# Entry of a two-block transformer kernel: two narrow weight slots first, and the second token tile normed by VectorE

## The reference, cut to what matters

```python
hn = rms_norm(h, norm_g[0])           # h = x, 512 tokens x 1024
...                                   # hn @ ev_w_in[0], cut in columns: q, k, v, gate, u, gate
u = hn @ ev_w_in[0][:, 1280:1792]     # 512 columns, the input of the state-space part
```

## Time and profile before

| | us |
|---|---|
| median of 3 runs | 1859.51 |
| lowest and highest run | 1858.56, 1860.19 |
| the profiled execution | 1856.27 |
| its span, first to last instruction | 1854.5 |

### The profile page before, as it was taken

The page is one execution under the profiler, slowest core; times in us unless marked ns, Lnnn a source line. Parts: engine busy times, 40 slices in busy tenths (PEclk is TensorE's granted clock), DMA queues, the critical chain, the costliest instruction groups (busy, mean ns, idle before and its releaser), DMA issues.

```text
span 1854.5 us, 24422 instructions
## 1 busy us (share of the span) xinstructions
PE 1780.5 (96%) x9572; PEld 1409.0 (76%) x9572; DVE 960.3 (52%) x1928; ACT 513.7 (28%) x1144; POOL 1015.7 (55%) x1051
## 2 busy tenths in 40 slices
PE   7778899999899999999999999999999999999998
PEld 6565668767668877778888888887667798888886
DVE  5849575488453345443564156434566356514642
ACT  3430453321442344442111021122434321101111
POOL 7406145656316574335776677655343377667762
PEclk9889899999999999999999999999999999999999
DMA  6121311322123321112332333222112133233321
GB/s 183 35 69 46 114 46 55 117 69 80 40 69 115 102 92 51 64 47 67 112 108 86 100 105 91 80 91 91 46 46 69 46 105 112 85 95 105 91 94 54
DMA packets 173058, 151.68 MB, mean 82 GB/s; under 512 B 9304, under 2 KB 148056, under 8 KB 172944
## 3 DMA queue, kind: packets, MB, share of 16 engines
q1 hardware_dynamic: 172400, 149.69, 26.5%
q10 hardware_dynamic: 544, 0.44, 0.1%
HBM read 147.97 MB, written 2.14 MB: 81 GB/s over the span
## 4 chain that ended last, share of the span: by engine, by line
PE 86%; DVE 5%; ACT 1%; issue 1%; DVEq 0%; ACTq 0%
PE ps L279 72%; PE ps L1932 2%; PE ps L1965 2%; PE ps L1950 2%; PE ps L1431 1%; PE ps L350 1%; PE ps L1409 1%; DVE s_tmp L1110 1%; PE ps L1908 1%; PE ps L1938 1%; PE ps L1352 1%; PE ps L1360 1%; PE ps L1368 0%; PE ps L1421 0%; PE ps L741 0%
## 5 line engine op out<-in xcount | busy, mean ns | idle before, releaser
L127 POOL TENSOR_SCALAR w_hi<-w_raw 128x512 fp32r<-128x512 f32 x522 | 314.7, 629 | 795.7 <-PE ps L279 732.8
L131 POOL TENSOR_TENSOR w_lo<-w_raw,w_hi 128x512 fp32r<-128x512 f32 x522 | 695.6, 1364 | 11.2
L279 PE MATMUL ps<-x_hi,w_hi 128*128 128x512 f32 (+1 forms) x1448 | 539.1, 372 | 0.7 <-DVE x_lo L432 0.7
L279 PE MATMUL ps<-x_hi,w_lo 128*128 128x512 f32 (+1 forms) x1448 | 528.9, 365 | 0.0
L279 PE MATMUL ps<-x_lo,w_hi 128*128 128x512 f32 (+1 forms) x1448 | 528.7, 365 | 0.0
L279 PEld LDWEIGHTS ps<-x_hi,w_hi 128*128 128x128 f32 x1448 | 275.3, 190 | 71.3 <-issue 21.7
L279 PEld LDWEIGHTS ps<-x_hi,w_lo 128*128 128x128 f32 x1448 | 275.1, 190 | 44.1
L279 PEld LDWEIGHTS ps<-x_lo,w_hi 128*128 128x128 f32 x1448 | 275.5, 190 | 40.5 <-issue 0.5
L2226 DVE SCALAR_TENSOR_TENSOR ffn_cv<-ps,col,ffn_cv 128x510 f32<-128x510 f32 (+1 forms) x176 | 131.8, 749 | 192.8 <-ACT ffn_cv L2204 188.1
L2204 ACT ACTIVATE ffn_cv<-ps,col 128x512 f32<-128x512 f32 x88 | 63.7, 775 | 500.2 <-PE ps L279 500.2
L307 DVE TENSOR_TENSOR h<-h,ps 128x512 f32<-128x512 f32 x64 | 43.9, 688 | 263.3 <-PE ps L279 263.3
(11 more groups left out here) (326 smaller groups left out, 2454.2 us busy)
## 6 DMA issues: line engine op xcount, KB each, us to landing
w_raw<-w_up SPq DMA_DIRECT2D x88, 512.0 KB, 5.1
w_raw<-w_down SPq DMA_DIRECT2D x16, 1024.0 KB, 5.0
w_raw<-od_w_in SPq DMA_DIRECT2D x12, 1024.0 KB, 5.2
w_raw<-w_in_fox SPq DMA_DIRECT2D x10, 1024.0 KB, 5.3
w_raw<-w_in_dil SPq DMA_DIRECT2D x10, 1024.0 KB, 5.1
w_raw<-ev_w_in SPq DMA_DIRECT2D x8, 1024.0 KB, 7.5
w_raw<-w_out SPq DMA_DIRECT2D x8, 1024.0 KB, 5.0
w_raw<-w_down SPq DMA_DIRECT2D x8, 768.0 KB, 4.4
```

Of the source, the lines that this page charges most:

```text
L127: ins = pool.tensor_scalar(hi[:, c:min(c + PIECE, size)], raw[:, c:min(c + PIECE, size)], 1.0, 1.0, ALU.mult, ALU.mult)
L131: ins = pool.tensor_tensor(lo[:, c:min(c + PIECE, size)], raw[:, c:min(c + PIECE, size)], hi[:, c:min(c + PIECE, size)].bitcast(F32), ALU. ...
L279: mm = pe.matmul(o, l, r, start=start and i == 0, stop=stop and i == 2)
```

## The change

Five things change, all at the entry.

1. The 512 columns of u are cut into three slots: 128, 128 and 256 columns (0.5, 0.5 and 1 MB). All later slots have numbers one higher.
2. `Seam` loses its case of the entry; a class `Entry` of its own takes its place. PE's order in it: transposes of tiles 0 and 1, slot 0 and slot 1 with half 0, transposes of tiles 2 and 3, slot 2 with half 0, then slots 0, 1 and 2 with half 1.
3. Tile 1 is squared, summed and scaled by DVE; ACT does its root, and tiles 0, 2 and 3. ACT does not wait for `col` before its first square, but after scaling tile 0, and makes the high parts of half 0 before it norms tiles 2 and 3. DVE inverts for tile 2 after all low parts of half 0.
4. The bias tables are made by DVE after the inverse of tile 2 and ahead of that of tile 3, no longer first. PE waits for them only before slot 2.
5. SP issues slots 0 and 1 together, ahead of x tiles 2 and 3. Slot 2 is in the call that follows the wait for `brow_ready` and the two stores.

```diff
-        w_ev_u = wide(ev, AW + 256 + 512, 512)
+        u0 = AW + 256 + 512
+        w_ev_u = [wide(ev, u0, 128), wide(ev, u0 + 128, 128), wide(ev, u0 + 256, 256)]
...
+            def tensor(self, pe, banks_free):
+                self.turn(pe, 0)
+                self.turn(pe, 1)
+                for i in range(2):
+                    pe.wait_ge(W.split_done, w_ev_u[i] + 1)
+                    self.begin(pe, w_ev_u[i], (4 + i,), 0)
+                self.turn(pe, 2)
+                self.turn(pe, 3)
+                pe.wait_ge(W.split_done, w_ev_u[2] + 1)
+                pe.wait_ge(banks_free, 1)
+                self.begin(pe, w_ev_u[2], (6, 7), 0)
+                for i in range(2):
+                    self.begin(pe, w_ev_u[i], (4 + i,), 1).then_inc(W.used, 1)
+                self.begin(pe, w_ev_u[2], (6, 7), 1).then_inc(W.used, 1)
...
+                squared(0)
+                rooted(0)
+                act.wait_ge(self.second_squared, 1)
+                rooted(1)
+                scaled(0)
+                act.wait_ge(cols_in, 16)
+                hi(0)
+                for tile in (2, 3):
+                    squared(tile)
+                    rooted(tile)
+                    scaled(tile)
+                hi(1)
...
+                dve.wait_ge(self.arrived[1], 16)
+                second = self.normed[:, 1, :]
+                dve.tensor_tensor_reduce(out=second, in0=h[:, 1, :], in1=h[:, 1, :], scale=1.0, scalar=0.0, op0=ALU.mult, op1=ALU.add,
+                                         accum_out=seam_stat[:, 0, 1:2]).then_inc(self.second_squared, 1)
+                inverse(0)
+                inverse(1)
+                dve.wait_ge(self.inverted.s, self.inverted.at(2))
+                dve.wait_ge(self.second_squared, 1)
+                dve.tensor_scalar(second, h[:, 1, :], seam_stat[:, 2, 1:2], None, ALU.mult).then_inc(self.second_scaled, 1)
+                dve.wait_ge(cols_in, 16)
+                for k in range(4):
+                    high_low(k, 0)
+                for k in range(4, KD):
+                    low(k, 0)
+                inverse(2)
+                between()
+                inverse(3)
...
                 for i in range(2):
                     sp.dma_start(h[:, i, :], t["x"][0][i * P:(i + 1) * P, :]).then_inc(self.x_in[i], 16)
-                W.load(sp, -RAW - SPLIT + 1)
+                W.load(sp, -RAW - SPLIT + 2)
                 for i in range(2, T):
                     sp.dma_start(h[:, i, :], t["x"][0][i * P:(i + 1) * P, :]).then_inc(self.x_in[i], 16)
                 self.load_more(sp)
-                W.load(sp, -RAW - SPLIT + 2)
                 sp.wait_ge(self.brow_ready, 1)
...
                 pe.wait_ge(self.ident_in, 16)
-                pe.wait_ge(self.brow_ready, 1)
-                self.first.begin_all(pe, w_ev_u, (4, 5, 6, 7))
+                self.first.tensor(pe, self.brow_ready)
...
-                act.wait_ge(self.cols_in, 16)
-                self.first.scalar(act)
+                self.first.scalar(act, self.cols_in)
...
-                self.first.vector(dve)
+                self.first.vector(dve, self.cols_in, bias_tables)
```

More of the change, by code:

```diff
@@ L331, in block_kernel, with __init__ @@
         class Seam:
-            def __init__(self, out_, gain, banks, normed, arrived=None):
-                self.out, self.gain, self.banks, self.normed, self.arrived = out_, gain, banks, normed, arrived
+            def __init__(self, out_, gain, banks, normed):
+                self.out, self.gain, self.banks, self.normed = out_, gain, banks, normed
                 self.rooted, self.inverted, self.scaled = tally("norm_rooted", T), tally("norm_inverted", T), tally("norm_scaled", T)
@@ L396, in scaled @@
                 def scaled(tile):
[L397 to L400, removed]
+                    act.wait_ge(self.out.added.s, self.out.added.at(4 + tile + 1))
                     if tile >= 2:
@@ L440, in add @@
                 def add(tile):
-                    if self.out is not None:
-                        self.out.add(dve, 1, tile)
+                    self.out.add(dve, 1, tile)
                 for tile in range(2):
@@ L457, in vector, with __init__, turn, scalar @@
                 low(7, 0)
+                inverse(3)
+                for k in range(4):
+                    high_low(k, 1)
+                for k in range(4, KD):
+                    low(k, 1)
+        class Entry(Seam):
+            def __init__(self, gain, banks, normed, arrived):
+                self.gain, self.banks, self.normed = gain, banks, normed
+                self.rooted, self.inverted, self.scaled = tally("norm_rooted", T), tally("norm_inverted", T), tally("norm_scaled", T - 1)
+                self.turned, self.hi_ready, self.x_ready = tally("norm_turned", 8), tally("norm_hi", 8), tally("norm_x", 2 * KD)
+                self.arrived, self.second_squared, self.second_scaled = arrived, sem("entry_squared"), sem("entry_scaled")
+            def turn(self, pe, tile):
+                if tile == 1:
+                    pe.wait_ge(self.second_scaled, 1)
+                else:
+                    pe.wait_ge(self.scaled.s, self.scaled.at(max(tile, 1)))
+                for k in range(KD):
+                    mm = pe.transpose(self.bank(k)[:, (tile % 2) * P:(tile % 2) * P + P], self.normed[:, tile % 2, k * P:(k + 1) * P],
+                                      ident[:, :])
+                    if tile % 2 == 1 and k % 2 == 1:
+                        mm.then_inc(self.turned.s, 1)
+            def tensor(self, pe, banks_free):
[12 more added lines that the diff above has]
+                self.begin(pe, w_ev_u[2], (6, 7), 1).then_inc(W.used, 1)
+            def scalar(self, act, cols_in):
+                link = linker(act, act_link)
+                def squared(tile):
+                    act.wait_ge(self.arrived[tile], 16)
+                    if tile >= 2:
+                        act.wait_ge(self.turned.s, self.turned.at(4 if tile == 3 else 1))
+                    link(act.activation(self.normed[:, tile % 2, :], h[:, tile, :], ACT.Square, accum_out=seam_stat[:, 0, tile:tile + 1]))
+                def rooted(tile):
+                    act.activation(seam_stat[:, 1, tile:tile + 1], seam_stat[:, 0, tile:tile + 1], ACT.Sqrt, scale=1.0 / D,
+                                   bias=eps_col[:, 0:1]).then_inc(self.rooted.s, 1)
+                def scaled(tile):
+                    act.wait_ge(self.inverted.s, self.inverted.at(tile + 1))
+                    act.activation(self.normed[:, tile % 2, :], h[:, tile, :], ACT.Copy,
+                                   scale=seam_stat[:, 2, tile:tile + 1]).then_inc(self.scaled.s, 1)
+                def hi(half):
+                    for k in range(4, KD):
+                        act.wait_ge(self.turned.s, self.turned.at(4 * half + k // 2 + 1))
+                        act.activation(self.x(x_hi, k, half), self.bank(k), ACT.Copy,
+                                       scale=col[:, self.gain + k:self.gain + k + 1]).then_inc(self.hi_ready.s, 1)
+                squared(0)
[10 more added lines that the diff above has]
+                hi(1)
+            def vector(self, dve, cols_in, between):
+                link = linker(dve, dve_link)
+                def inverse(tile):
+                    dve.wait_ge(self.rooted.s, self.rooted.at(tile + 1))
+                    dve.reciprocal(seam_stat[:, 2, tile:tile + 1], seam_stat[:, 1, tile:tile + 1]).then_inc(self.inverted.s, 1)
+                def low(k, half):
+                    if k >= 4:
+                        dve.wait_ge(self.hi_ready.s, self.hi_ready.at(4 * half + (2 if k < 6 else 4)))
+                    gain = col[:, self.gain + k:self.gain + k + 1]
+                    dve.scalar_tensor_tensor(self.x(x_lo, k, half), self.bank(k), gain, self.x(x_hi, k, half).bitcast(F32),
+                                             ALU.mult, ALU.subtract).then_inc(self.x_ready.s, 1)
+                def high_low(k, half):
+                    dve.wait_ge(self.turned.s, self.turned.at(4 * half + k // 2 + 1))
+                    link(dve.tensor_scalar(self.x(x_hi, k, half), self.bank(k), col[:, self.gain + k:self.gain + k + 1], None, ALU.mult))
+                    low(k, half)
+                dve.wait_ge(self.arrived[1], 16)
[8 more added lines that the diff above has]
+                dve.wait_ge(cols_in, 16)
+                for k in range(4):
+                    high_low(k, 0)
+                for k in range(4, KD):
+                    low(k, 0)
+                inverse(2)
+                between()
@@ L524, in __init__ @@
                 self.x_in = [sem(f"a_x_in{i}") for i in range(T)]
-                self.first = Seam(None, C_NORM_G, (0, 1, 2, 3), self.normed, self.x_in)
+                self.first = Entry(C_NORM_G, (0, 1, 2, 3), self.normed, self.x_in)
                 b = []
-                for slot in range(2):
-                    for j in range(2):
```

(11 more changed lines are left out.)

4 lines of the change are left out of this document (removed).

## The result

| | before | after |
|---|---|---|
| median of 7 runs each, us | 1860.19 | 1866.47 |
| lowest, highest | 1855.89, 1861.29 | 1862.45, 1868.47 |
| profiled execution, its span | 1856.27, 1854.5 | 1867.37, 1865.2 |

The ratio is 1.0033, with a 95% interval of 1.0022 to 1.0043: 4 to 8 us slower. Forecast were 7.6, and 6.3 came. In absolute terms 1867.1 was forecast and 1866.47 measured; that this is closer than the difference is luck, since the median of before over seven runs is 0.7 above the median over three that the sum started from.

What follows compares the result with a forecast made beforehand. TensorE, busy 96% of the span, was taken as the bound. Restart at 32.8, 144 matmuls (17.35) and 2.3 of slow clock put q at 52.45, 7.6 us later: 1867.1 us, range +5.4 to +10.7, with cases 1862.5 to 1870.5.

Steps and rivals of the forecast that it cites:

- the sum: Start of q: 52.45 against 44.82 before, 7.6 us later, passed on to the total: 1859.51 + 7.6 = 1867.1.
- Part 1: Norm at the entry: ScalarE no longer waits for the gains, VectorE does tile 1; half 0 ready 4.3 us earlier.
- rival A: ScalarE's first square: the gains did not hold it, so it stays at 9.7; +10.6 us, 1870.1; chance 0.07.
- Part 2: Narrow slots 0 and 1: splits end at 12.2 and 16, ahead of x; 48 matmuls done 3 to 5 us earlier.
- Part 3: Slot 2 behind the bias tables on SyncE: issued 20.1, landed 25.3, split 32.8; TensorE idles about 10 us.
- Part 4: TensorE's restart after idling: half-level clock costs 1.7 to 2.9 us, 2.3 taken.
- The term before the change: TensorE's first weight matmuls from 18.05 in the kernel before: half-level clock cost 1.9 us, included in its 44.82.
- The thin cover: GpSimd's split of the first q slot: ends at 51.3, 1.2 us ahead of need, against about 12 before.
- The lock: VectorE and GpSimd's shared ports: constants could cost GpSimd 0.2 each, sum 8.6; by the profile rows it stays 7.6.
- B: TensorE's restart and after 67.8: warm restart or slack takes back part of the loss; +5.3 or +3.0 us; chance 0.10.
- C: Wait at 67.8: VectorE's constants set the pace, hiding TensorE's shift and passing on their lead; 1855.2 us; chance 0.04.

Runs made afterwards that it cites:

- e12: Changed kernel with ScalarE's wait for the gains put back ahead of its first square, as before; 1870.21 us, one run.
- e7: Changed kernel with ScalarE norming tile 1 again instead of VectorE, all else as changed; 1866.49 us, one run.
- e1: Changed kernel with the load of slot 2 issued ahead of SyncE's wait for the bias tables; 1861.31 us, ratio to before 1.0007.
- e2: Changed kernel with VectorE's bias tables right behind its scaling of tile 1, ahead of the high parts, SyncE's order untouched; 1860.71 us, one run.
- e3: Changed kernel with SyncE waiting for the two bias stores to land before it loads slot 2; 1868.66 us, one run.
- e4: Changed kernel with TensorE doing slots 0 and 1 with half 1 before it waits for slot 2; 1867.7 us, ratio to before 1.0040.
- e5: Changed kernel with slot 2 loaded ahead of the bias wait and slots 0 and 1 with half 1 before slot 2; 1863.66 us, ratio to before 1.0012.
- e11: Changed kernel with slots 0 and 1 with half 1 before slot 2, and ScalarE's two sines behind the second q unit; 1866.34 us, one run.
- e6: Changed kernel with two u slots of 256 columns as before, the second loaded ahead of the wait; 1860.63 us, ratio to before 1.0000.

## Why the prediction was right

**Part 1.** First square 5.25 forecast, 5.29 measured; reduction 1.3 and 1.23 with its accumulator read beside it; transposes 9.4 and 9.52; high parts 11.9 and 11.99. The scaling on VectorE was bounded at 1.9 and took 0.75. Right in size, and e12 shows that the gains had held ScalarE, which rival A doubted. That VectorE's part cost nothing holds; what wasn't said is that it gains nothing either once the wait for the gains has moved (e7). With that wait back in its old place the first high part is 3.35 later (e12), most of the 4.1 that the change won there.

**Part 2.** First weight matmul 12.9 forecast, 13.18 measured; half 0 was done at 20.9, just ahead of the 21 to 23 given. Right as a result, less so in the reading: GpSimd began slot 0 at 9.36, not 8.5, and had it split at 13.13, not 12.2. So the split was not ahead of x, whose first low part was done at 12.99; it ended last here too, by 0.1.

**Part 3.** Issue 20.1 forecast, 19.69 measured; landing 25.3 and 25.08; restart 32.8 and 32.51. e1, e2, e3 and e12 show the chain at each link: with the load moved to 13.4 the loss goes, with it moved by 1.10 the marks move by 1.08 and 1.15. This was the term that decided, and it is shown.

**Part 4.** The half-level stretch was priced at 2.3. It lasted 3.99 us at 0.50 and cost (51.71 - 32.51) less 144 x 0.1205 = 1.85. That is the mis-sized term, 0.45 of the 0.7 by which the sum of 7.6 missed the 6.9 in the trace; the restart's 0.3 is the rest. The experiments restart the same 144 matmuls after other waits, and the same subtraction gives 2.36 in e1 (3.50 us idle before it), 1.53 in e2 (3.73), 1.92 in e3 (11.13), 1.37 in e7 (10.24) and 1.42 in e12 (10.18). So the length of the idle time does not order the cost, three of six lie under the 1.7 that was the lower bound, and the miss of 0.45 is within what one execution differs from another. The term before the change has a weak spot: that before paid 1.9 from 18.05 on is read from the distance of the starts, 0.213, while the granted clock of that stretch reads 1.00:

```profile
18.05:22.45 4.40, 4.40 (x20) 4.40 (x21) 3.60 (x10) 4.06 (x9) 4.32 (x6) 1.00 0.71 231
```

The starts decide here, since they are what the sum is made of.

**The sum.** 6.9 at q, 6.7 at the late transposes, 6.3 between medians, where 7.6 was forecast. The thin cover held: GpSimd had the first q slot split at 50.91, 0.8 ahead of TensorE, where 1.2 was forecast. VectorE's constants began at 27.21, where 28 to 30 was said, and cost nothing, as said: ScalarE ran the sines at 44.11 and had to wait for TensorE after that.

**The lock.** Three of VectorE's small instructions between 28.8 and 32.5 took 1.19 each, where they take 0.17 alone, and GpSimd's four subtractions beside them took 4.93 (from 27.52 on), against 4.95 at 13.05 before. The sum by the rows was the right one. The Trainium skill (SBUF — State Buffer, "SBUF: two separate sides") has the later of the two engines blocked, whichever it is. VectorE's side of that is seen here; the 0.2 for each constant that GpSimd was to lose by it is not. With VectorE's products of 128x512 beside it GpSimd does lose: four subtractions took 6.16 at 61.29.

**Rivals.** A and B did not come. C has its truth elsewhere: VectorE's constants do set the pace as soon as TensorE is early rather than late (e4, e5, e11). The prediction put the hand-over at the tables; when TensorE is early, the first to hand it over is ScalarE's queue, which keeps a bank from TensorE's fourth q unit (e4, e5).

Left open: what the stretches of lower clock in the odd layer hang on, and whether the usual execution of before has them. One of 7 runs of the changed kernel was at 0.985 and the others at 0.982 to 0.983, but idle time at the entry lowers that mean too.

## What to carry to other kernels

When an instruction is moved on one engine, follow what waits for it on the queues that issue transfers: here 1.7 us of table work, which no compute engine missed where it was put, held a 1 MB load, its split and all matmuls behind it. When a wait is filled or removed, look for the next in-order queue on the way, since 7 us gained on TensorE came out as nothing until ScalarE's sines and GpSimd's early splits were moved as well. Work that is not needed for 30 us should not run beside a serial chain of another engine that it stretches, as GpSimd's splits stretched VectorE's constants from 0.17 to 1.19 us each.

## What was not expected of the hardware

SyncE needed 4.29 us to issue x tiles 2 and 3 in the changed kernel, where it had needed 1.19 before. Both weight slots ahead of them now have rows of 512 bytes rather than 1024, so twice the packets stand in the queue for the same bytes (the profile counts 174098 packets in all, 173058 before). Before, and with wide slots again (e6), where it was 1.35:

```profile
2.11 1.19 SPq L562 DMA_DIRECT2D h<-x  x2
```

```profile
2.11 1.35 SPq L665 DMA_DIRECT2D h<-x  x2
```

It cost nothing here, since nobody waits for the five tables behind them; with something urgent there, 3 us would have been the price of narrow slots (an estimate, 4.29 less 1.19 or 1.35). That the row length is the cause, rather than the second slot in front, is not separated by these runs.

The bias stores, 20 KB each, landed within 1.3 us of the end of the last issue (e3), where 2 us had been put.
